# Small products of a chunked linear recurrence spread over the four quarters of the matrix engine

## The reference, cut to what matters

```
def step(state, inp):
    r_t, w_t, k_t, v_t, kk_t, a_t = inp
    sk = einsum('bhvk,bhk->bhv', state, kk_t)
    state = (state * w_t[:, :, None, :]
             - sk[..., None] * (a_t * kk_t)[:, :, None, :]
             + v_t[..., None] * k_t[:, :, None, :])
    return state, einsum('bhvk,bhk->bhv', state, r_t)
...
bonus = sum(r_h * k_h * r_k, axis=-1, keepdims=True) * v_h
y = (norm(y) * lnx_g + lnx_b + bonus) * g
```

## Time and profile before

| | us |
|---|---|
| median of 3 runs | 2774.73 (2771.67 to 2776.4) |
| profiled execution, device time | 2772.68 |
| its span in the trace | 2771.1 |
| outside the span | 1.58 |
| PE busy | 2713.1 (98%) |
| DVE, ACT, POOL busy | 1590.7, 987.9, 192.3 |
| granted PE clock, mean | 0.996 |
| the two recurrence parts, 1232.8 to 1384.1 and 2043 to 2200.9 | some 310 |

### The profile page before, as it was taken

How to read it: one execution, slowest core, us unless ns; L and a number is a source line. 1 busy time by engine, 2 the same in 40 slices (tenths; PEclk the granted TensorE clock), 3 DMA queues, 4 the chain that set the end, 5 groups by cost and what they waited for, 6 DMA issues and landing times.

```text
span 2771.1 us, 45647 instructions
## 1 busy us (share of the span) xinstructions
PE 2713.1 (98%) x19357; PEld 2258.5 (82%) x19357; DVE 1590.7 (57%) x2331; ACT 987.9 (36%) x1362; POOL 192.3 (7%) x272
## 2 busy tenths in 40 slices
PE   8999999999999999999999999999999999999999
PEld 7878888898688888877878888888868878888887
DVE  6668777864667777665563553333585454633334
ACT  5643212344632222353332431223444333422223
POOL 5000000000000000001050000000010220000000
PEclk9999999999999999999999999999999999999999
DMA  4333555522046555220023223232220123232231
GB/s 158 107 114 123 186 168 177 161 77 77 9 129 186 161 173 170 90 91 27 4 81 107 92 92 106 92 99 86 78 71 4 33 91 103 80 103 95 93 101 65
DMA packets 238830, 281.18 MB, mean 101 GB/s; under 512 B 9646, under 2 KB 225202, under 8 KB 238642
## 3 DMA queue, kind: packets, MB, share of 16 engines
q1 hardware_dynamic: 225322, 226.28, 25.1%
q0 software_dynamic: 13184, 52.11, 6.3%
q10 hardware_dynamic: 136, 0.03, 0.0%
HBM read 276.30 MB, written 2.10 MB: 100 GB/s over the span
## 4 chain that ended last, share of the span: by engine, by line
PE 89%; DVE 5%; ACT 2%; issue 2%; POOL 1%; DMA 0%; SPq 0%; DVEq 0%; ACTq 0%; POOLq 0%
PE psum L2517 25%; PE psum L2518 25%; PE psum L2519 24%; DVE wlo L1619 1%; PE psum L2597 1%; PE psum L2599 1%; PE psum L2598 1%; PE psum L3085 1%; PE psum L3070 1%; PE psum L3053 1%; PE psum L3109 1%; PE psum L2531 1%; PE psum L3042 1%; POOL mo L857 0%; ACT whi L909 0%
## 5 line engine op out<-in xcount | busy, mean ns | idle before, releaser
L2517 PE MATMUL psum<-hh,whi 128*128 128x512 f32 (+1 forms) x2032 | 787.6, 388 | 4.4 <-DVE wlo L1619 4.4
L2518 PE MATMUL psum<-hl,whi 128*128 128x512 f32 (+1 forms) x2032 | 778.4, 383 | 0.0
L2519 PE MATMUL psum<-hh,wlo 128*128 128x512 f32 (+1 forms) x2032 | 778.2, 383 | 0.0
L1619 DVE TENSOR_TENSOR wlo<-raw,whi 128x2048 fp32r<-128x2048 f32 x219 | 506.4, 2312 | 462.3 <-ACT whi L909 461.9
L909 ACT ACTIVATE whi<-raw 128x2048 fp32r<-128x2048 f32 x219 | 418.2, 1910 | 521.3 <-PE psum L2519 517.3
L2517 PE MATMUL psum<-mh,whi 128*128 128x512 f32 (+1 forms) x1248 | 485.7, 389 | 1.4 <-issue 1.1
L2518 PE MATMUL psum<-ml,whi 128*128 128x512 f32 (+1 forms) x1248 | 479.4, 384 | 0.0
L2519 PE MATMUL psum<-mh,wlo 128*128 128x512 f32 (+1 forms) x1248 | 479.3, 384 | 0.0
L2517 PEld LDWEIGHTS psum<-hh,whi 128*128 128x128 f32 x2032 | 382.7, 188 | 92.0 <-issue 8.2
L2519 PEld LDWEIGHTS psum<-hh,wlo 128*128 128x128 f32 x2032 | 382.5, 188 | 75.1
L2518 PEld LDWEIGHTS psum<-hl,whi 128*128 128x128 f32 x2032 | 382.8, 188 | 73.0 <-issue 0.5
(11 more groups left out here) (470 smaller groups left out, 2748.1 us busy)
## 6 DMA issues: line engine op xcount, KB each, us to landing
rest<-in_ada_w POOLq DMA_DIRECT2D x64, 768.0 KB, 5.3
raw<-in_w_gu SPq DMA_DIRECT2D x44, 1024.0 KB, 5.0
raw<-in_w_in SPq DMA_DIRECT2D x34, 1024.0 KB, 5.1
raw<-in_w_mlp_in SPq DMA_DIRECT2D x32, 1024.0 KB, 5.4
raw<-in_w_mlp_out SPq DMA_DIRECT2D x32, 1024.0 KB, 5.2
raw<-in_w_out SPq DMA_DIRECT2D x16, 1024.0 KB, 5.1
raw<-in_w_down SPq DMA_DIRECT2D x16, 1024.0 KB, 4.8
raw<-in_w_mem_kv SPq DMA_DIRECT2D x8, 1024.0 KB, 5.1
```

Source lines behind the costliest of these rows:

```text
L1619: ins = dve.tensor_tensor(wlo[:, g % 2, :, :], raw[:, g % 2, :, :], f32(whi[:, g % 2, :, :]), ALU.subtract)
L2517: pe.matmul(out, whi_, xhi, start=first, stop=False)
L2518: pe.matmul(out, whi_, xlo, start=False, stop=False)
L2519: return pe.matmul(out, wlo_, xhi, start=False, stop=last)
```

## The change

1. `AkkV`, `TF`, `WU`, `WT`, `Ark` and `Arb` are issued as 16 products each on four quarters (`AkkV` had 16 before, on two). `TF` is turned by products with the identity, by `turned`. `WT` takes two banks instead of one.
2. The copies follow: `AkkV` in four ACT passes with a head stride instead of two, negated; `TF` still in four; `WU` in four passes of 64 partitions x 512 instead of four of 128 x 256; `WT` in two instead of one; each mask of `Ark` and `Arb` in four DVE passes of 64 x 256 instead of two of 128 x 512, which write only the diagonal blocks. The others are zeroed once a layer, by a new POOL memset of 128 x 2048.
3. The bonus: four products of 128x128 with 512 columns (`bon`) become `head_sums` (four products with 32 output partitions each, job `bs`, before `level_right` of n = 3 at m = 0), a copy by ACT, and `head_factors` (four products with 32 input partitions each) in the old place.
4. In the attention, 7 products of 128x128x128 without use (`idle_products`) are put between the scores and the turn in two of its steps (j = 8 and 12).

The diff, cut to its core (indentation shortened):

```
@@ -264,7 +264,7 @@
             self.pair("WU", l, p)
-            self.add("WT", l, p)
+            self.pair("WT", l, p)
...
@@ -282,6 +282,7 @@
                 self.block("v2", l, 1, 1, kept=True)
+                self.add("bs", l)
...
@@ -542,7 +543,7 @@
 AK = GS = carve(mo, 7 * T, 2, 4, CH)
-AR, AB = carve(mo, 4 * Q, 8, P), carve(mo, 5 * Q, 8, P)
+AR, AB, both_rows = carve(mo, 4 * Q, 8, P), carve(mo, 5 * Q, 8, P), carve(mo, 4 * Q, 2 * Q)
...
@@ -815,6 +816,7 @@
     q.step(pool.tensor_tensor(strict2[:, :], strict[:, 0:CH], strict[:, CH:P], ALU.add))
+    q.step(pool.tensor_tensor(incl[:, 0:CH], incl[:, 0:CH], incl[:, CH:P], ALU.add))
...
@@ -877,6 +879,7 @@
         pool.memset(MB, 0.0).then_inc(S("mb_zero"), 1)
+        pool.memset(both_rows, 0.0).then_inc(S("rows_zero"), 1)
@@ -1376,30 +1379,34 @@
                 ready(act, j)
-                free(act.activation(KA[s, 1, :], bank(j)[s, :], ACT.Copy), j)
+                for i in range(2):
+                    ins = act.activation(KA[s, 1, :].rearrange("p (t i n) -> p t i n", t=4, i=2)[:, :, i, :],
+                                         four(j)[HD * i:HD * i + HD], ACT.Copy, scale=-1.0)
+                free(ins, j)
 
         def inverse(m):
-            for i in range(2):
-                j = J["TF", l, m, i]
+            for c in range(2):
+                j = J["TF", l, m, c]
                 ready(act, j)
-                p = bank(j).rearrange("p (h n) -> p h n", h=4)
-                for c in range(2):
-                    s = slice(CH * c, CH * c + CH)
-                    ins = act.activation(MB[s, 4 * i:4 * i + 4, s], p[0:CH, :, s], ACT.Copy)
+                s = slice(CH * c, CH * c + CH)
+                for i in range(2):
+                    ins = act.activation(MB[s, 4 * i:4 * i + 4, s], four(j)[HD * i:HD * i + HD], ACT.Copy)
                 free(ins, j)
 
         def keys_values_solved(m):
-            for i in range(2):
-                j = J["WU", l, m, i]
+            for c in range(2):
+                j = J["WU", l, m, c]
                 ready(act, j)
                 p = bank(j).rearrange("p (j n) -> p j n", j=4)
-                act.activation(WU[:, 4 * i:4 * i + 4, 0:HD], p[:, :, 0:HD], ACT.Copy)
-                free(act.activation(WU[:, 4 * i:4 * i + 4, HD:P], p[:, :, HD:P], ACT.Copy, scale=-1.0), j)
+                for i in range(2):
+                    ins = act.activation(WU[CH * c:CH * c + CH, 4 * i:4 * i + 4, :], p[HD * i:HD * i + HD], ACT.Copy)
+                free(ins, j)
 
         def keys_turned(m):
-            j = J["WT", l, m]
-            ready(act, j)
-            free(act.activation(WT, bank(j).rearrange("p (j n) -> p j n", j=4), ACT.Copy), j)
+            for c in range(2):
+                j = J["WT", l, m, c]
+                ready(act, j)
+                free(act.activation(WT[:, :, CH * c:CH * c + CH], four(j), ACT.Copy), j)
 
         def state_inputs(m):
@@ -1444,6 +1451,9 @@
             if m == 0:
+                j = J["bs", l]
+                ready(act, j)
+                free(act.activation(HR, bank(j), ACT.Copy), j)
                 own_part("v2", 1, 1, c0 + 11, v_dst[:, 3, :])
@@ -2220,8 +2224,16 @@
         def rows_masked(m, name, dst):
+            if m == 0 and name == "Ark":
+                dve.wait_ge(S("rows_zero"), l + 1)
             for i in range(2):
-                masked(name, m, i, dst, incl)
+                j = J[name, l, m, i]
+                ready(dve, j)
+                for c in range(2):
+                    s = slice(CH * c, CH * c + CH)
+                    ins = dve.tensor_tensor(dst[s, 4 * i:4 * i + 4, s], pc4(j)[s],
+                                            bc(incl[:, 0:CH])[s], ALU.mult)
+                free(ins, j)
 
         def state_step(m, c):
 
@@ -2872,6 +2884,8 @@
                         fox_scores(j)
+                    if j in (8, 12):
+                        idle_products(7, "fox_t", l, j - 2, 0)
                     if 2 <= j < PAIRS + 2:
                         fox_turn(j - 2, 0)
@@ -3028,7 +3031,8 @@
                         s = chunk[c]
-                        ins = pe.matmul(p[c][s, head(i, t)], AK[s, i, t, :], VT[m % 2][s, head(i, t)], start=True, stop=True)
+                        ins = pe.matmul(p[c][half[i], t * HD:(t + 1) * HD], AK[s, i, t, :], VT[m % 2][s, head(i, t)],
+                                        start=True, stop=True)
                         if (t, i) == (3, 1):
@@ -3044,9 +3048,9 @@
-        def turned(m, n):
-
-            p = [start("TR", l, m, n, c) for c in range(2)]
+        def turned(m, *name):
@@ -3091,11 +3095,7 @@
                 evacuated(pe, J["MLM", l, m, len(LEVELS) - 1, i])
-            for i in range(2):
-                p = start("TF", l, m, i)
-                for t in range(4):
-                    ins = pe.transpose(p[0:CH, t * P:(t + 1) * P], MM[m % 2][:, i, t, :], ident[:, :])
-                done(ins)
+            turned(m, "TF", l, m)
 
         def solve(m):
@@ -3103,20 +3103,27 @@
             evacuated(pe, J["tok", l, m, 0])
-            for i in range(2):
-                p = start("WU", l, m, i)
-                for t in range(4):
-                    ins = pe.matmul(p[:, t * P:(t + 1) * P], MB[:, 4 * i + t, :], KA[:, :, head(i, t)], start=True, stop=True)
-                done(ins)
-
-        def solve_turned(m):
-
-            p = start("WT", l, m)
+            p = [start("WU", l, m, c) for c in range(2)]
             for t in range(4):
                 for i in range(2):
-                    ins = pe.matmul(p[half[i], t * P:(t + 1) * P], KA[:, 0, head(i, t)], MB[:, 4 * i + t, :],
-                                    start=True, stop=True)
-            done(ins)
+                    for c in range(2):
+                        s = chunk[c]
+                        ins = pe.matmul(p[c][half[i], t * P:(t + 1) * P], MB[s, 4 * i + t, s], KA[s, :, head(i, t)],
+                                        start=True, stop=True)
+                        if (t, i) == (3, 1):
+                            done(ins)
+
+        def solve_turned(m):
+
+            p = [start("WT", l, m, c) for c in range(2)]
+            for t in range(4):
+                for i in range(2):
+                    for c in range(2):
+                        s = chunk[c]
+                        ins = pe.matmul(p[c][half[i], t * CH:(t + 1) * CH], KA[s, 0, head(i, t)], MB[s, 4 * i + t, s],
+                                        start=True, stop=True)
+                        if (t, i) == (3, 1):
+                            done(ins)
 
         def state_inputs(m):
@@ -3161,7 +3168,8 @@
 
-            evacuated(pe, J["WT", l, m])
+            for c in range(2):
+                evacuated(pe, J["WT", l, m, c])
@@ -3233,8 +3241,8 @@
             if m:
-                products("Ark", m - 1, K2, R2)
-                products("Arb", m - 1, A2, R2)
+                squares_of("Ark", m - 1, K2, R2)
+                squares_of("Arb", m - 1, A2, R2)
@@ -3244,6 +3252,8 @@
                 values_part(7, KT)
+                pe.wait_ge(S("bonus_in"), 4 * l + 4)
+                done(head_sums(start("bs", l), X2))
             if m:
                 state_step(m - 1, 1)
@@ -3252,10 +3262,9 @@
             if m == 0:
+                evacuated(pe, J["bs", l])
                 for t in range(4):
-                    pe.wait_ge(S("bonus_in"), 4 * l + t + 1)
-                    p = start("bon", l, t)
-                    done(pe.matmul(p, sum_64[:, :], X2[:, t, :], start=True, stop=True))
+                    done(head_factors(start("bon", l, t), t))
                 pe.wait_ge(S("rows_decayed"), 2 * l + 2)
             for x in range(3):
```

20 lines of the change are left out of this document (4 added, 16 removed).

## The result

The changed kernel takes 2780.35 us (median of 20 runs, 2775.7 to 2784.48), the kernel before beside it 2775.07 (2771.55 to 2778.82): ratio 1.0017, 95% interval 1.0012 to 1.0023, so 5 us slower (3 to 6). That is clear of the noise of these runs, and just inside the 0.2% under which the prediction called a change the same as none. The forecast was 2767, the range 2758 to 2773. Both are wrong, and so is the sign.

The account below looks back on a forecast made before the run. PE bounds the kernel (busy 2713.1 of 2771.1 us). Recurrence 10.8, bonus -0.8, idle products 1.2 and instructions -4.2 make 7.0 off 2772.68, so 2765.7; with half of 2.05 carried, 2767, range 2758 to 2773.

Parts of the forecast that it names:

- The idle products: Attention, before the turn: seven products fill a 1.33 us hole and keep the clock at 2.4 GHz; 1.2 us gained.
- `Ark` and `Arb`: Left of n = 2 to right of n = 3: of 0.90 us gained on PE, 0.3 a tile remains, between 0 and 0.9.
- the term of the masks: DVE's `Arb` masks, which `TR` of n = 3 awaits: four passes take 1.4 us where two took 1.28.
- The instructions: PE's queue: 88 more records a tile bring 0.7 us more holes per pass, six passes: -4.2, bounds 0 and -9.
- rival 3: Recurrence passes: instruction supply becomes the bound, so the kernel is slower; 7 us more a layer, 2787; chance 0.05.
- the floor of 1.58: From `level_right` to the next `level_left`: PE waits for DVE's `MM`, leaving 0.07 of `WT`'s 0.47 us gain.
- `WU`'s banks: First `TR` of n = 1 waits for four ACT passes: 0.54 us each tile of m = 1 to 3; 0.34 of 0.88 remains.
- the bonus's wait: Before `level_right` of n = 4, second layer: PE's wait for DVE to free the bonus bank grows from 2.48 to about 4 us.
- The second sign of being wrong: The forecast is wrong if the second layer's part from the first `solve` on shrinks by less than 1 us.
- Rival 1: PE's instruction pieces cost nothing new: 11.2 us gained, 2761.5, or 2753 if bank and mask waits also fail to come; chance 0.22.
- Rival 2: Waits take all: holes of 1.2 us more per pass and `bs` at full price; 2.6 gained, 2770; chance 0.18.
- Rival 4: A longer bonus hole before `level_right` of n = 4 lowers the clock in both layers: 1 to 2 us more, 2768; chance 0.1.

Follow-up runs that it names:

- run 1: The changed kernel without its idle products in the attention: ratio 1.0003 to the kernel before, 0.9986 to the changed kernel.
- Run 6: The changed kernel with its attention idle products in the other, free bank of the turn: ratio 0.9992 to the kernel before.
- Run 9: The kernel before, products unchanged, with each `Ark` and `Arb` mask in four DVE passes of 64x256, plus the memset: ratio 1.0016.
- run 3: The kernel before with only `Ark` and `Arb` on four quarters, their masks in four DVE passes and the memset: ratio 1.0018.
- run 5: The kernel before with three blocks of unused products near its end, to measure instruction supply: no ratio; the first block takes 33.6 us.
- runs 10, 11: The kernel before plus unused products ahead of `Ark` in every pass: 32 records in the former (ratio 1.002), 4 records in the latter (1.0001).
- run 7: The kernel before with only `AkkV` and `WU` on four quarters and the shorter bonus: ratio 1.0001.
- run 8: The kernel before with only the shorter bonus (`bs`, `head_sums`, `head_factors`): ratio 1.0003.
- Run 15: The kernel before with attention idle products in the free bank, plus 5 more ahead of the first RWKV-7 layer's projection `lat`: ratio 0.9986.

## Why the prediction was wrong

**The idle products, forecast +1.2, measured -4 (run 1).** This step failed outright. "Seven products are 7 x 0.235 = 1.65, so 0.3 longer than the hole" supposes that they start at the hole's start. They write the bank of the turn and so wait for it; the earlier trace rows name the releaser, DVE L2026, and L2026 is what frees a bank, not what makes the probabilities. Run 6 shows the gain in another bank. 5 of the 13 us between 2767 and 2780.35 are here; 7 are the recurrence and the bonus, below, and 1.4 are the level of the kernel before, 2773.7 as carried in the sum and 2775.07 beside the changed kernel.

**`Ark` and `Arb`, forecast +0.3 a tile, measured 5 slower in all.** Two things. First the term of the masks, 1.4 for 1.28, is 1.75. "A pass of 64x256 is not in these rows for DVE" was true of the group and not of the trace: two operations ahead of `Ark`'s masks it has L2235 and L2239 with 64x256 at 0.41 to 0.43. I scaled with the free size, and half the partitions take no less time. Run 9 prices the masks at 4 (2 to 7). Second, 32 more records at a place that has two groups of 32 on either side: run 3's "issue" holes grew by 8.5, while PE's busy time fell by 3.9. Runs 3 and 9 don't divide the 5 more sharply than their intervals.

**The instructions, forecast -4.2 with bounds 0 and -9.** The mechanism was right, and rival 3 had it as the bound; the size was off. The spacing of a piece, 3.7, was read right (run 5: 3.5 to 4.0). I averaged over the pass, where 3.9 a piece lies just above it, and took 0.7 a pass. But the queue evens out only some 270 records (run 5). Where the change is dense, from the left of n = 2 to `U`, a record costs some 31 ns (runs 10, 11), 1.0 us for 32, as much as the 0.90 that spreading `Ark` and `Arb` saves. The "issue" holes grew by 14.1, more than my far bound of 9. One thing is left open: the longest such hole of before, 2.28 at 1273.51, stands behind four microseconds in which the DMA was busy to 0.98 and 1.03, and run 5 measures a piece on idle queues. Whether a piece takes longer beside other transfers was not tried.

**What held.** The groups' own times (`WU` 0.92, the others 0.5); the floor of 1.58; `WU`'s banks, 0.54 forecast, 0.25 to 0.43 measured in four of six passes of the changed kernel and 0.49 to 0.54 in all six of run 7; ACT's 2.42; the bonus's wait "about 4", 3.48, and its loss of 0.8, which run 8 (+1, within 2.5) doesn't contradict. The recurrence was to give 5.8 with all terms (10.8 - 0.8 - 4.2); by run 1 it costs 1. Of that 7, the masks are 4, and the rest fits the supply. How it divides among `AkkV`, `TF`, `WU` and `WT` stays open: each is within 1 of nothing by its run, and together they are 1.7 with an interval of 3.5. A part that adds no record (`AkkV`) still reaches the next piece sooner and may wait for it; that this ate its gain was not shown.

**The signs named ahead.** Of those listed, the groups' times, the start of `TR` and its releaser came as said. "About 4 us in sum" of more issue holes was 14, and the attention had its hole and its half clock: these two refute the forecast, in the two terms above. The second sign of being wrong came too: the second layer's part from the first `solve` to the last group of `Y` was to shrink by 1 us or more and grew by 0.8 (117.5 to 118.3). The chance of 0.05 for rival 3 was too low, because its test was put on the average of a pass. Rival 1, that pieces cost nothing new, is refuted by runs 5 and 10. Rival 2 had the waits for `WU`'s banks at the place where they came, but not the masks. Rival 4, the clock behind the bonus's wait, came in the first layer: behind the wait of 1.91 the granted clock is 0.51 from 1273 to 1275 and 0.64 from 1275 to 1277, where before it is 1.00, and the eight records of L3019 take 1.41 for 1.16. In the second layer it is low in both (0.55 and 0.60 before, 0.50 and 0.75 after). Its share of the loss, 1 to 2 by the prediction, was not measured by itself.

## What to carry to other kernels

Count PE's records as well as its time: in run 5 128 of them came no faster than every 3.5 us, 27 to 31 ns each, once the first 270 were used up, so spreading a group over four quarters can pay only where what lies around it is slower than that. Price a copy or mask by the instruction, not by its partitions, and look in the trace for the same shape on the same engine before scaling one. A filler fills a hole only if it doesn't wait for what made the hole: put it into a bank that is free by then. Run 15 shows that even this doesn't keep the clock up everywhere.
